# The pooling branch of a hybrid encoder kernel: channels on partitions, shifted sums on GpSimd, map folded into the output weights

## The chip, the core and the metric

The kernel runs on one core of a Trainium2 chip. A core has five engines that run their own instruction streams and meet at semaphores: TensorE (PE, with its weight loads shown as PEld), VectorE (DVE), ScalarE (ACT), GpSimd (POOL) and SyncE (SP), which here only issues transfers. The metric is the device time of one execution in microseconds (us), less is better.

## What is computed

Two layers over 2048 tokens of 1024 channels, float32. Each layer adds a mixing block and an expert block to x. The mixing block has three branches side by side: attention (512 channels), pooling (256) and retention (256), from one projection of h. The pooling branch is what the change is about:

```python
def multiscale_pool(u, pool_w, pool_scale):          # u = the 256 pooling channels of the projection
    cs = jnp.cumsum(uf, axis=1)
    for gi, w in enumerate(POOL_WINDOWS):            # 2, 4, 8, 16: one window for each 64 channels
        shifted = jnp.pad(c, ((0, 0), (w, 0), (0, 0)))[:, :s]
        mean = (c - shifted) / jnp.minimum(t1, float(w))
        outs.append(mean - uf[..., sl])
    y = jnp.einsum('bsgc,gce->bsge', d, pool_w).reshape(b, s, POOL_WIDTH)
    return y * pool_scale

x = x + jnp.einsum('bse,ed->bsd', concatenate([y_a, y_b, y_c]), w_out[l])   # reference, l = layer
x = x + moe_ffn(rms_norm(x, norm_ffn[l]), ...)       # 32 experts, 2 for each token
```

So each pooling channel gets the mean of its last w tokens minus the token itself, then a 64 x 64 map for each group, then a scale, and then its rows of w_out.

## The kernel before

Each layer has a mixing part and an expert part. The **mixing part** goes over 16 tiles of 128 tokens in 18 steps (`steps`): 0 and 1, a hardware loop of six passes over two steps each (2 to 13), then 14 to 17. Step s holds three strands, each a block of code in every engine's stream, woven by hand: *front* projects tile s, *back* mixes tile s-1, *tail* routes tile s-2. `b` is the parity of s, `o` the other one. Nothing but the written order and the semaphores sets what runs when.

TensorE in a full step, in its order: transposes of q, k and the rotated retention heads (`tr`, helper line 1126, which waits for `rank_read`, `qk_ready` and `rope_ready`); `chunk(0)`, the first 512 columns of the projection, as 8 products of hT (stationary) with `win`, line 1151; scores (1201, 1210, 1214); transposes of the routed tile; `chunk(1)`, columns 512 to 1023: k and v in its first 256, the pooling channels u in its last 256; router products (1225); half of `chunk(2)`; the router's fold (1230); retention state (1237); **the pooling bands** (1247 to 1251): u as the stationary operand, with a constant band matrix of window means minus identity as the moving one, `pool_cur` for this tile and `pool_prev` for the last 15 tokens of the tile before, kept in `upv`; retention's inner product (1257, end `pe_ykv`); the other half of `chunk(2)`; transposes of the probabilities; **the pooling map** (1269) after `kvd_read`; half of `chunk(3)`; attention's product with v (1282); transposes of the retention output; rest of `chunk(3)`; the output projection (1305), 8 products for each half k of the 1024 columns, with the ranking products (1162, 1163) between the halves.

VectorE copies the band products to `dT` (line 896), and ScalarE the map's output to `mixT` with the scale (line 713), which ends in `pool_ready`. ScalarE evicts each chunk to `proj`, with the token's normalization `rf` as its scale (lines 679, 691, 705, 717); tokens lie on partitions there. VectorE's rest of the step goes: `kv`, `rstd` (a reciprocal root in 12 short instructions, lines 778 to 789) and z for retention, `route` (962 to 998), `ycT`, squares, `rstd` and scaling for q and k (916 to 924), x addition of half 0 (938), hT of the next tile (818), `place` (1005 to 1018, with `rank_read` at its end), x addition of half 1.

GpSimd does yc (545) when z is ready, six rotary operations (556 to 562), the copy of the tile's last u rows to `upv` (565), at whose end `rope_ready` stands, the copies of v to `v0w` (570, 572), and later the two indirect writes of slots (580), when `slots_ready` has come.

At a layer's start SyncE loads constants (layer 1 only), x, the small parameters, the four parts of w_in, w_out and the next x tiles in one queue. The **expert part** works through 32 experts with all weights streamed; it is the same in both kernels.

## Time and profile before

| | |
|---|---|
| median of 3 runs | 3359.57 us (3357.9 to 3360.9) |
| profiled execution | 3360.36 us, span 3358.6 us |
| TensorE busy | 3213.6 us, 96% |
| VectorE, ScalarE, GpSimd busy | 1488.1, 596.2, 1072.1 us |
| mean granted TensorE clock | 0.979 |
| mixing parts | from 16.37 to about 880 us and from about 1690 to 2550 us |

The span is the time between the first and the last instruction of the profiled execution. In a timeline row stand the start in us from the span's start, the duration, the engine, the line in kernel.py, the operation, output and inputs with their shapes, how many instructions are merged in the row, and in brackets how long the engine was idle before it and what ended that. A float32 product of the program shows as two TensorE instructions. `<-issue` is idle time in which the engine waited for nothing that the profile shows. DVEq, SPq and the like are an engine's instruction queue.

### The profile page before, as it was taken

The page shows a single profiled execution, that of the slowest core. Times are in us where ns is not written, and L with a number is a line of the kernel's source. Part 1 is how long each engine was busy: PE and PEld are TensorE (multiplying, and loading weights), DVE is VectorE, ACT ScalarE, POOL GpSimd, SP SyncE. Part 2 cuts the span into 40 slices and gives each one's busy share as a digit, 9 for nine tenths or more (in the row PEclk, how much of TensorE's full clock was granted, in tenths as well). Part 3 has the DMA queues.
Part 4 walks back from the last instruction along what each step waited for, and adds up shares of the span by engine and source line. Part 5 has one row for each costly group of instructions (what it writes and reads, how often), then busy time and mean ns, then how long its engine had stood idle before and what let it go on. Part 6 is the DMA issues. An engine that isn't in the chain of part 4 may idle for free.

```text
span 3358.6 us, 58551 instructions
## 1 busy us (share of the span) xinstructions
PE 3213.6 (96%) x19892; PEld 2412.3 (72%) x19892; DVE 1488.1 (44%) x4766; ACT 596.2 (18%) x1738; POOL 1072.1 (32%) x1088
## 2 busy tenths in 40 slices
PE   7999999999699999999889999999986999999998
PEld 3555555554499999999845555555554999999998
DVE  3666666666322222222246666666653222222221
ACT  1222222222111111111112222221220111111111
POOL 1111111111155455554310111111111555555543
PEclk9999999999799999999999999999987999999999
DMA  8212112121388899999842122121123889999996
GB/s 281 70 35 69 51 53 69 35 69 64 149 285 280 297 321 328 334 348 341 283 141 70 41 63 69 35 69 59 45 110 147 251 280 319 307 340 334 333 342 189
DMA packets 228590, 613.55 MB, mean 183 GB/s; under 512 B 63724, under 2 KB 120556, under 8 KB 195388
## 3 DMA queue, kind: packets, MB, share of 16 engines
q1 hardware_dynamic: 165724, 527.54, 43.3%
q0 software_dynamic: 62592, 82.75, 11.3%
q8 instruction: 124, 2.03, 0.2%
q14 instruction: 150, 1.23, 0.1%
HBM read 530.95 MB, written 80.35 MB: 182 GB/s over the span
## 4 chain that ended last, share of the span: by engine, by line
PE 84%; DMA 5%; DVE 3%; issue 3%; SPq 1%; DVEq 1%; POOL 1%; ACT 1%; POOLq 0%; ACTq 0%
PE bank L1151 24%; PE bank L1337 23%; PE bank L1365 15%; PE bank L1305 13%; DMA arena<-hrows,arena 3%; PE bank L1126 3%; PE bank L1257 1%; DVE arena L1071 1%; PE bank L1282 1%; PE bank L1201 1%; PE bank L1210 1%; DMA arena<-in_x 1%; PE bank L1225 0%; POOL arena L618 0%; ACT arena L743 0%
## 5 line engine op out<-in xcount | busy, mean ns | idle before, releaser
L1337 PE MATMUL bank<-arena,wts 128*128 128x135 f32 (+6 forms) x8192 | 1022.9, 287 | 3.3 <-ACTq L736 3.3
L1337 PEld LDWEIGHTS bank<-arena,wts 128*128 128x128 f32 x8192 | 1016.6, 191 | 3.5 <-issue 3.5
L1151 PE MATMUL bank<-wts,arena 128*128 128x512 f32 x2048 | 917.7, 597 | 39.5 <-DVE arena L818 20.3
L1151 PEld LDWEIGHTS bank<-wts,arena 128*128 128x128 f32 x2048 | 376.3, 191 | 452.1 <-issue 427.6
L625 POOL DMA_INDIRECT out<-arena x316 | 502.4, 1590 | 157.9 <-issue 89.6
L1365 PE MATMUL bank<-arena,wts 128*128 128x135 f32 (+6 forms) x4096 | 519.4, 287 | 14.7 <-DVE arena L1104 14.3
L1365 PEld LDWEIGHTS bank<-arena,wts 128*128 128x128 f32 x4096 | 511.5, 191 | 18.1 <-issue 18.0
L1305 PE MATMUL bank<-wts,arena 128*128 128x512 f32 x1024 | 454.8, 597 | 0.1
L1071 DVE STREAM_TRANSPOSE arena<-arena 128x256 f32<-128x256 f32 x304 | 135.4, 446 | 559.6 <-DMA arena<-hrows,arena 538.1
L1305 PEld LDWEIGHTS bank<-wts,arena 128*128 128x128 f32 x1024 | 192.9, 191 | 231.8 <-issue 215.6
L618 POOL DMA_INDIRECT arena<-hrows,arena x304 | 294.6, 969 | 183.2 <-issue 163.1
L545 POOL TENSOR_TENSOR arena<-arena 128x256 f32<-128x256 f32 x32 | 23.1, 723 | 950.2 <-DVEq L907 950.2
L1085 DVE STREAM_TRANSPOSE arena<-bank 128x480 f32<-128x480 f32 (+4 forms) x192 | 104.2, 593 | 475.9 <-PE bank L1365 475.9
L743 ACT ACTIVATE arena<-arena,tab 128x256 f32<-128x256 f32 x316 | 133.1, 496 | 616.5 <-DVEq L1086 616.5
L580 POOL DMA_INDIRECT table<-pay,sloti x64 | 63.7, 995 | 457.0 <-DVE sloti L1018 447.2
L613 POOL TENSOR_TENSOR arena<-tab,quarter 128x5 int32<-128x5 int32 (+2 forms) x64 | 12.3, 192 | 426.4 <-DMA tab<-table 377.8
L751 ACT ACTIVATE arena<-bank 128x270 f32<-128x270 f32 (+6 forms) x64 | 26.3, 412 | 649.5 <-PE bank L1337 649.5
L1126 PEld LDWEIGHTS bank<-cst,arena 128*128 128x128 f32 x896 | 103.0, 143 | 44.8 <-issue 38.3
L1126 PE MATMUL bank<-cst,arena 128*128 128x128 f32 x896 | 125.5, 281 | 2.5 <-DVE arena L938 1.6
L722 ACT ACTIVATE arena<-arena 128x1024 bf16<-128x1024 f32 x32 | 33.8, 1056 | 443.3 <-DVE arena L938 443.3
L938 DVE TENSOR_TENSOR arena<-arena,bank 128x512 f32<-128x512 f32 x64 | 44.0, 688 | 116.5 <-PE bank L1305 106.3
L686 ACT ACTIVATE arena<-bank,stat 128x128 f32<-128x128 f32 x256 | 89.8, 380 | 28.2 <-DVEq L864 28.2
(173 smaller groups left out, 2402.1 us busy)
## 6 DMA issues: line engine op xcount, KB each, us to landing
wts<-in_w_gate SPq DMA_DIRECT2D x128, 1024.0 KB, 8.0
wts<-in_w_up SPq DMA_DIRECT2D x128, 1024.0 KB, 10.3
wts<-in_w_down SPq DMA_DIRECT2D x128, 1024.0 KB, 14.7
hrows<-arena SPq DMA_DIRECT2D x36, 512.0 KB, 3.0
out<-arena SPq DMA_DIRECT2D x36, 512.0 KB, 2.7
arena<-in_x SPq DMA_DIRECT2D x32, 512.0 KB, 5.1
wts<-in_w_in SPq DMA_DIRECT2D x8, 2048.0 KB, 15.7
arena<-out SPq DMA_DIRECT2D x32, 512.0 KB, 4.4
```

What stands on the lines that cost most here:

```text
L580: e.indirect_dma_start(table, bass.IndirectOffsetOnAxis(ap=sloti[b][:, k:k + 1].bitcast(U32), axis=0), pay[b][:, 2 * k:2 * k + 2], None).t ...
L618: e.indirect_dma_start(xg[b][:, g * PIECE:(g + 1) * PIECE], None, hpieces, bass.IndirectOffsetOnAxis(ap=piece[:, i, g:g + 1].bitcast(U32), ...
L625: e.indirect_dma_start(opieces, bass.IndirectOffsetOnAxis(ap=piece[:, i, g:g + 1].bitcast(U32), axis=0), ysb[b][:, g * PIECE:(g + 1) * PIE ...
L686: a(pr[:, k, g], (bC, bD)[k][:, g * P:(g + 1) * P], ACT.Exp, bias=stat[:, 16 + n:17 + n], scale=1.0, accum_out=stat[:, 24 + n:25 + n])
L743: a(y, y, ACT.Copy, scale=tab[:, i, g, 1:2].bitcast(F32)).then_inc(y_scaled, 1)
L1071: v.transpose(windows(xT_all[b], g * step, DC, 32 * GMAX, 32), x_piece)
L1085: v.transpose(y[:, 3 * k:3 * k + m], windows(bk, 0, m, w, w))
L1126: return nc.tensor.transpose(dst, src, ident[0:m, 0:m])
L1151: i = mm(bIP[n % 2][:, :], hT[:, d], win[:, n, d], start=(d == 0), stop=(d == DC - 1))
L1305: i = mm(bIP[k][:, :], mixT[:, d], wout[:, d, 512 * k:512 * k + 512], start=(n == 0), stop=(n == DC - 1))
L1337: return mm(gu_at(f, k, w), lhs, xT[:, d, 0:w], start=start, stop=(d == DC - 1), skip_group_check=True)
L1365: j = mm(dst, lhs, hTm[:, f, 0:w], start=(f == 0 and d % 3 == 0), stop=(f == FC - 1), skip_group_check=True)
```

## The change

In seven parts. (a) In chunk 1 the 256 pooling columns are no longer computed with tokens on partitions: for each of 8 slices d there is one product of 256 columns (k and v) and two of 128 with `win` stationary and hT moving, so that u comes out with channels on partitions, unnormalized. ScalarE copies it to `raw_uT`, after a new wait for `pool_ready` of the tile before, and evicts the other half to `proj`. (b) The normalization is per token, and so along the columns now: VectorE writes diag(rf) in place of an empty instruction, TensorE multiplies a matrix of ones with it, ScalarE copies the product to `rfb`. (c) GpSimd keeps 16 columns of the tile before, multiplies by rfb, adds shifted copies for windows 2, 4, 8 and 16, scales by 1/w and subtracts u; the result `dT` (now two) is what the output projection reads. (d) The band products, the map's products, the copies behind them and the copy to `upv` are gone. (e) VectorE multiplies the maps by the scale once a layer, TensorE multiplies them into rows 512 to 767 of w_out in step 1 (`fold`), and ScalarE writes the result over `wout` (`folded`). (f) The constants lose 1536 columns of 128 x 4 bytes and gain 34. (g) `logits4` gets a place of its own.

```diff
-for _name, _n in (("ident", P), ("before", P), ("ones", P), ("causal", P), ("pool_cur", 4 * P),
-                  ("pool_first", 4 * P), ("pool_prev", 4 * P), ("gamma", 2), ("fold", 32), ("rev8", 8),
+for _name, _n in (("ident", P), ("before", P), ("ones", P), ("causal", P),
+                  ("per_window", 2), ("early", 32), ("gamma", 2), ("fold", 32), ("rev8", 8),
...
@@ GpSimd, front
                         e.tensor_tensor(dst[:, :, 1], rtmp[:, 2], rtmp[:, 3], ALU.add)
-                        e.drain()
-
-                        e.tensor_copy(upv[b][96:128, :], proj[b][96:128, U0:U0 + UW]).then_inc(rope_ready, 1)
-                        e.drain()
+                        e.drain().then_inc(rope_ready, 1)
 
                         if back:
                             wait_alone(e, pe_pv, t0)
                         e.tensor_copy(v0w[b][0:64, :], proj[b][0:64, V0:V0 + KVW])
                         e.drain()
                         e.tensor_copy(v0w[o][64:128, :], proj[b][64:128, V0:V0 + KVW]).then_inc(vw_ready, 1)
+                        e.drain()
+
+                        if isinstance(s, int) and s == 0:
+                            e.memset(uT[:, :, 0:16], 0.0)
+                        else:
+                            e.tensor_copy(uT[:, :, 0:16], uT[:, :, P:P + 16])
+                        e.drain()
+                        wait_alone(e, rfb_ready, t0 + 1)
+                        e.tensor_tensor(uT[:, :, 16:], raw_uT, rfb.unsqueeze(1).to_broadcast([P, 2, P]), ALU.mult)
+                        e.drain()
+                        e.tensor_tensor(sums[:, :, 1:], uT[:, :, 1:], uT[:, :, 0:P + 15], ALU.add)
+                        e.drain()
+                        e.tensor_tensor(sums2[:, :, 3:], sums[:, :, 3:], sums[:, :, 1:P + 14], ALU.add)
+                        e.drain()
+                        e.tensor_tensor(sums[:, 1, 7:], sums2[:, 1, 7:], sums2[:, 1, 3:P + 12], ALU.add)
+                        e.drain()
+                        e.tensor_tensor(sums2[64:128, 1, 15:], sums[64:128, 1, 15:], sums[64:128, 1, 7:P + 8], ALU.add)
+                        e.drain()
+                        for ph, total in ((slice(0, 64), sums), (slice(64, P), sums2)):
...
+                            e.tensor_tensor(dT[b][ph], total[ph, :, 16:],
+                                            const("per_window", ph.start, ph.stop).unsqueeze(2).to_broadcast([64, 2, P]), ALU.mult)
+                        e.drain()
+                        e.tensor_tensor(dT[b], dT[b], uT[:, :, 16:], ALU.subtract).then_inc(pool_ready, 1)
                         e.drain()
@@ ScalarE
+                def folded(j):
+
+                    e.wait_ge(pe_fold, l * 2 + j + 1)
+                    for k in range(2):
+                        a(wout[:, 4 + j, 512 * k:512 * k + 512], (bA, bB)[k][:, :], ACT.Copy)
+                    e.drain().then_inc(fold_ready, 1)
...
                         a(proj[b][:, 0:512], bIP0[:, :], ACT.Copy, scale=rf[b]).then_inc(proj_ready, 1)
+                        if isinstance(s, int) and s == 1:
+                            folded(0)
...
                         e.wait_ge(proj_psum, t0 * 4 + 2)
-                        a(proj[b][:, 512:1024], bIP1[:, :], ACT.Copy, scale=rf[b]).then_inc(proj_ready, 1)
+                        if not isinstance(s, int) or s > 0:
+                            e.wait_ge(pool_ready, t0)
+                        a(raw_uT.rearrange("p j n -> p (j n)"), bIP1[:, 256:512], ACT.Copy)
+                        a(proj[b][:, 512:768], bIP1[:, 0:256], ACT.Copy, scale=rf[b]).then_inc(proj_ready, 1)
+                        if isinstance(s, int) and s == 1:
+                            folded(1)
...
                     if front:
+                        e.wait_ge(pe_rfb, t0 + 1)
+                        a(rfb, bA[:, 384:512], ACT.Copy).then_inc(rfb_ready, 1)
                         e.wait_ge(proj_psum, t0 * 4 + 3)
...
-                        e.wait_ge(pe_lin, t0)
-                        for j in range(2):
-                            a(mixT[:, 4 + j], bB[:, j * P:(j + 1) * P], ACT.Copy, scale=pscale[:, j:j + 1])
-                        e.drain().then_inc(pool_ready, 1)
@@ VectorE
-                e.nop().then_inc(rf_ready, 1)
+                v.tensor_scalar(diag[b], ident, rf[b], None, ALU.mult).then_inc(rf_ready, 1)
...
+                v.tensor_tensor(pw, pw, bc(pscale.unsqueeze(2), [P, 2, P]), ALU.mult).then_inc(maps_ready, 1)
...
-                        v.tensor_copy(dT, bB[:, 256:512].rearrange("p (j n) -> p j n", j=2))
@@ TensorE
-                        for d in range(*part):
-                            i = mm(bIP[n % 2][:, :], hT[:, d], win[:, n, d], start=(d == 0), stop=(d == DC - 1))
+                        if n == 1:
+                            for d in range(DC):
+                                mm(bIP1[:, 0:256], hT[:, d], win[:, 1, d, 0:256], start=(d == 0), stop=(d == DC - 1),
+                                   skip_group_check=True)
+                                for j in range(2):
+                                    i = mm(bIP1[:, 256 + P * j:384 + P * j], win[:, 1, d, 256 + P * j:384 + P * j], hT[:, d],
+                                           start=False, stop=(d == DC - 1), skip_group_check=True)
+                        else:
+                            for d in range(*part):
+                                i = mm(bIP[n % 2][:, :], hT[:, d], win[:, n, d], start=(d == 0), stop=(d == DC - 1))
...
+                    def fold(j):
+
+                        e.wait_ge(wout_full, (l + 1) * 16)
+                        e.wait_ge(maps_ready, l + 1)
+                        if j > 0:
+                            e.wait_ge(fold_ready, l * 2 + j)
+                        for k in range(2):
+                            i = mm((bA, bB)[k][:, :], pw[:, j], wout[:, 4 + j, 512 * k:512 * k + 512], start=True, stop=True)
+                        i.then_inc(pe_fold, 1)
+
                     chunk(0)
+                    if first:
+                        fold(0)
...
                     chunk(1)
+                    if first:
+                        fold(1)
...
+                    if front:
+                        if first:
+                            e.wait_ge(fold_ready, l * 2 + 2)
+                        e.wait_ge(rf_ready, t0 + 1)
+                        mm(bA[:, 384:512], ones, diag[b], start=True, stop=True).then_inc(pe_rfb, 1)
...
-                        wait_alone(e, kvd_read, t0)
-                        for j in range(2):
-                            i = mm(bB[:, P * j:P * j + P], pw[:, j], dT[:, j], start=True, stop=True)
-                        i.then_inc(pe_lin, 1)
...
-                                i = mm(bIP[k][:, :], mixT[:, d], wout[:, d, 512 * k:512 * k + 512], start=(n == 0), stop=(n == DC - 1))
+                                i = mm(bIP[k][:, :], dT[o][:, d - 4] if d in (4, 5) else mixT[:, d], wout[:, d, 512 * k:512 * k + 512], start=(n == 0), stop=(n == DC - 1))
```

TensorE's order in a full step of the loop, from the router products to the second half of chunk 2 and to the pooling map, before and then after (the line numbers of after are its own):

```order
L1225 MATMUL bank<-arena,par 32x128 x8
L1149 ISA
L1151 MATMUL bank<-wts,arena 128x512 x4
L1230 MATMUL bank<-cst,arena 128x32
L1237 MATMUL bank<-arena 64x64 x4
L1249 MATMUL bank<-cst,arena 64x128 x2
L1251 MATMUL bank<-cst,arena 64x128 x2
L1249 MATMUL bank<-cst,arena 64x128 x2
L1251 MATMUL bank<-cst,arena 64x128 x2
L1257 MATMUL bank<-arena 128x64 x4
L1151 MATMUL bank<-wts,arena 128x512 x4
L1126 MATMUL bank<-cst,arena 128x128 x8
```

```order
L1183 MATMUL bank<-arena,wts 128x128 x2
L1275 MATMUL bank<-arena,par 32x128 x8
L1177 ISA
L1187 MATMUL bank<-wts,arena 128x512 x4
L1284 MATMUL bank<-arena,cst 128x128
L1286 MATMUL bank<-cst,arena 128x32
L1292 MATMUL bank<-arena 64x64 x4
L1299 MATMUL bank<-arena 128x64 x4
L1187 MATMUL bank<-wts,arena 128x512 x4
L1154 MATMUL bank<-cst,arena 128x128 x8
L1177 REGISTER_ALU
```

The eight band products (1249, 1251) are gone, the product of ones with diag (1284) stands ahead of the router's fold, and chunk 1 ends in products of 128 columns (1183).

GpSimd's order in the same step, from the last rotary operation to the writes of slots, before and then after:

```order
L561 TENSOR_TENSOR arena<-arena 128x8x32
L562 TENSOR_TENSOR arena<-arena 128x8x32
L565 COPY arena<-arena 32x256
L570 COPY arena<-arena 64x128
L572 COPY arena<-arena 64x128
L331 REGISTER_ALU
L580 DMA table<-pay,sloti 69888x2 x2
```

```order
L554 TENSOR_TENSOR arena<-arena 128x256
L559 COPY arena<-arena 64x128
L561 COPY arena<-arena 64x128
L567 COPY arena<-arena 128x2x16
L324 REGISTER_ALU
L570 TENSOR_TENSOR arena<-arena 128x2x128
L572 TENSOR_TENSOR arena<-arena 128x2x143
L574 TENSOR_TENSOR arena<-arena 128x2x141
L576 TENSOR_TENSOR arena<-arena 128x137
L578 TENSOR_TENSOR arena<-arena 64x129
L585 TENSOR_TENSOR arena<-arena,cst 64x256 x2
L588 TENSOR_TENSOR arena<-arena 128x256
```

Nine operations and one wait (for `rfb_ready`) now stand between the v0w copies and the writes of slots, and the copy of u's last rows (565) is gone.

## Rows read from the trace of the kernel before

**Rows 1.** Windows: stretch, busy us (instructions) of PE, PEld, DVE, ACT, POOL, clock, DMA, GB/s

```profile
1780.00:1900.00 120.00, 119.93 (x544) 62.80 (x543) 80.69 (x284) 30.93 (x101) 15.75 (x24) 1.00 0.19 57
```

**Rows 2.** Timeline, TensorE, a full step: start us, us, engine, line, op, shapes, count, idle

```profile
421.64 7.03 PE L1151 MATMUL bank<-wts,arena 128*128 128x512 f32 x16
...
432.95 0.45 PE L1237 MATMUL bank<-arena 128*64 128x64 f32 x8
433.23 0.39 PE L1249 MATMUL bank<-cst,arena 128*64 128x128 f32 x4
...
434.20 1.10 PE L1257 MATMUL bank<-arena 128*128 128x64 f32 x8
...
439.51 0.61 PE L1269 MATMUL bank<-arena,par 128*128 128x128 f32 x4
439.96 3.60 PE L1151 MATMUL bank<-wts,arena 128*128 128x512 f32 x8
...
455.45 7.11 PE L1305 MATMUL bank<-wts,arena 128*128 128x512 f32 x16
```

**Rows 3.** Timeline, TensorE, expert part, then the page's weight loads (mean ns)

```profile
1575.96 7.38 PE L1365 MATMUL bank<-arena,wts 128*128 128x128 f32 x64 [0.26 <-DVE arena L1104]
1583.18 14.46 PE L1337 MATMUL bank<-arena,wts 128*128 128x128 f32 x128
...
L1337 PEld LDWEIGHTS bank<-arena,wts 128*128 128x128 f32 x8192 | 1016.6, 191 | 3.5 <-issue 3.5
```

**Rows 4.** Timeline, GpSimd, the same step as rows 2

```profile
440.37 0.72 POOL L545 TENSOR_TENSOR arena<-arena 128x256 f32<-128x256 f32 x1 [29.46 <-DVEq L907]
...
460.74 1.02 POOL L580 DMA_INDIRECT table<-pay,sloti  x1 [13.69 <-DVE sloti L1018]
```

**Rows 5.** Timeline, VectorE: the same step, loop's edge first; last two: step 16

```profile
418.83 0.69 DVE L842 COPY arena<-bank 128x512 f32<-128x512 f32 x1 [2.47 <-issue]
...
441.23 0.58 DVE L969 TENSOR_TENSOR arena<-arena 128x16 f32<-128x16 f32 x1
...
445.69 0.17 DVE L981 TENSOR_SCALAR arena<-arena 128x8 f32<-128x8 f32 x1
...
459.43 0.19 DVE L1016 CUSTOM_DVE_ANT_0 arena<-arena 128x32 f32<-128x32 f32 x1
...
849.69 0.17 DVE L969 TENSOR_TENSOR arena<-arena 128x16 f32<-128x16 f32 x1
...
852.33 0.17 DVE L981 TENSOR_SCALAR arena<-arena 128x8 f32<-128x8 f32 x1
```

**Rows 6.** Timeline, VectorE and then GpSimd, step 0 of layer 1; last: rows 2's step

```profile
41.96 1.13 DVE L921 TENSOR_TENSOR arena<-arena,stat 128x512 f32<-128x512 f32 x1
...
42.51 1.17 POOL L559 TENSOR_TENSOR arena<-arena 128x256 f32<-128x256 f32 x1
...
455.09 0.69 DVE L921 TENSOR_TENSOR arena<-arena,stat 128x512 f32<-128x512 f32 x1
```

**Rows 7.** Timeline, ScalarE, eviction of chunk 1 in the step of rows 2

```profile
428.71 0.69 ACT L691 ACTIVATE arena<-bank,stat 128x512 f32<-128x512 f32 x1 [1.48 <-PE bank L1151]
```

**Rows 8.** Timeline, TensorE, step 16 of layer 1

```profile
840.39 0.64 PE L1249 MATMUL bank<-cst,arena 128*64 128x128 f32 x4
...
842.24 1.54 PE L1257 MATMUL bank<-arena 128*128 128x64 f32 x8
```

**Rows 9.** Timelines, TensorE, ScalarE, TensorE; then transfers from 0 to 150 us

```profile
66.59 3.70 PE L1151 MATMUL bank<-wts,arena 128*128 128x512 f32 x8 [2.75 <-ACT arena L679]
...
64.82 1.06 ACT L656 ACTIVATE arena<-arena 128x1024 bf16<-128x1024 f32 x1 [15.86 <-DMA arena<-in_x]
...
1720.76 0.66 PE L1126 MATMUL bank<-cst,arena 128*128 128x128 f32 x4 [0.92 <-POOL arena L565]
...
GB/s 158 296 347 387 387 386 387 320 317 386 407 413 409 415 418 405 263 172 11 0 0 9 0 2 0 0 25 115 251 276 106 0 2 0 0 4 0 0 2 0
...
cst<-in_consts SPq DMA_DIRECT2D x1, 1154.0 KB, 5.4
```

52 lines of the change are left out of this document (18 added, 34 removed).

## Prediction

> **What bounds the kernel now.** I read the windows first, to see which engine has no room, then TensorE's timeline of one step of the mixing part, then VectorE's and GpSimd's at the same place, then the ends of each layer. In 120 us in the middle of layer 2's mixing part TensorE is busy for 119.93, at a granted clock of 1.00, that is 2.4 GHz, and the DMA share is 0.19 [rows 1]. So in this part a microsecond taken off TensorE is a microsecond of time, as long as no other engine is late. The mixing part has 18 steps per layer: step s projects tile s ("front"), mixes tile s-1 ("back") and routes tile s-2 ("tail"). Fourteen per layer (s = 2 to 15) are the full kind that rows 2 show, 28 in all. The expert part holds nothing that the change touches; it starts when the mixing part's chain is through, so it only moves.
>
> **What leaves TensorE, per full step.** The pooling band products start at 433.23, and the products after them (line 1257) at 434.20 [rows 2]: four groups like the first, 0.22 each by their spacing, 0.88, plus 0.09 of a gap before line 1257, which I leave standing. The pooling map (line 1269) starts at 439.51 and the next work at 439.96: 0.45 [rows 2]. Together -1.33.
>
> **What comes to TensorE, per full step.** Chunk 1 had 8 products of 512 columns, each shown as two instructions, 16 in 7.03 us: 0.439 each [rows 2]. Now it is 16 instructions of 256 columns and 32 of 128, the same number of columns, but three weight loads where there was one. A 128-column instruction with a fresh weight load takes (1583.18 - 1575.96) / 64 = 0.113 in the expert part [rows 3]. No row shows 256 columns; the line between 0.113 and 0.439 gives 0.221. Sum 16 x 0.221 + 32 x 0.113 = 7.15, so +0.12. Bounds: nothing, if columns alone count; at most 32 x (0.191 - 0.113) = +2.5 more, if each short instruction had to wait for a whole weight load, whose own mean is 0.191 [rows 3]. I stay at +0.12, because rows 3 are the very same shape and hide the load. The product of ones with diag adds two 128-column instructions, 0.23. In all -1.33 + 0.12 + 0.23 = **-0.98 per full step, 28 times: -27.4**.
>
> **GpSimd and VectorE.** GpSimd loses one small copy, which `rope_ready` had to wait for, and gains nine operations behind the v0w copies, from about 446.5 on. A TENSOR_TENSOR of 256 columns takes 0.72 [rows 4]; taking a fixed 0.17 or so and the rest by columns (my estimate), those of 286, 282, 137 and 129 columns cost 0.78, 0.77, 0.47 and 0.46; with four of 256 columns (the product with rfb, two scalings by 64 partitions, the subtraction) and the small copy it is 5.6 us, some 7 with the drains. GpSimd ends near 454, and its next wait, for slots, ends at 460.74 [rows 4]. The output products want dT one step later. GpSimd itself has room.
>
> What it does to VectorE is the dear question. Beside GpSimd's six rotary operations the routing from line 969 to line 981 takes 445.69 - 441.23 = 4.46 us; alone, in the step without them, 852.33 - 849.69 = 2.64, of which about 0.33 is a gap without a releaser [rows 5]. So some 2.15 are lost to six operations, 0.36 each: an addition of 16 columns takes 0.58 instead of 0.17, ending with GpSimd's operation. It goes both ways: a product of VectorE takes 1.13 for 0.69, and GpSimd's beside it 1.17 for 0.72 [rows 6]. The Trainium skill, SBUF — State Buffer, section "SBUF: two separate sides", calls the port pair that these two share an exclusive lock held for the whole instruction; the trace agrees with that, and the GPSIMD Engine Reference, section 4.1, advises against elementwise work on GpSimd.
>
> Eight long operations at 0.36 are 2.9 us. Some of them will lie beside work that rows 5 do not have: a 0.8 us reduction and a copy from PSUM, which showed no stretch, and a 0.8 us square that loses at most one operation for its own length. Walking the two queues against each other by these rules I get 1.8 to 2.3; I take 2.3, with ends at 1.5 and at 5.6, where all of GpSimd's time is lost to VectorE.
>
> The cover is this. VectorE's last step of `place` ends at 459.62, and TensorE's second half of the output products, which starts at 455.45 and takes 7.11, ends at 462.5 [rows 2, 5]. That leaves 2.9. TensorE now reaches this point 0.45 earlier, and VectorE drops the dT copy, about 0.3, and has its 0.2 of diag at another place: **cover 2.7**. TensorE's next step opens with a wait for `rank_read`, behind which the transposes and chunk 0 are queued, so every microsecond beyond 2.7 would be paid, in each of 28 steps. At 2.3 nothing is. The picks for the ranking and hT for chunk 0 are further from being missed. Where the loop of two steps closes, VectorE stands 2.47 without a releaser at the back edge of the loop before line 842, and TensorE waits a few tenths for it [rows 5]; this chain hangs on the end of the output products and stays.
>
> **ScalarE.** It loses two activations for the map's output, gains the copy of rfb, and evicts chunk 1 in two halves, some 0.3 longer. It has 1.48 idle ahead of that eviction [rows 7], and the logits behind it are wanted by TensorE only after half of chunk 2. The new wait for `pool_ready` ahead of raw_uT's copy is over some 20 us earlier. Nothing on the path.
>
> **The ends.** Step 16 has no chunk to hide in, and its pooling products run at twice the time: from 840.39 to 842.24, 1.85 less the gap of 0.1, on the chain [rows 8]: -1.75 twice, **-3.5**. The map there lies beside VectorE's longer way to z and gives nothing. Layer 2: step 0 pays 0.12 + 0.23; step 1 saves 0.44 (half the bands), 0.45 and pays 0.35; the fold is four products of 512 columns, 4 x 0.88 = 3.5, and its evictions (four of 0.69, by the row of the same size in [rows 7]) lie beside chunk 2; the wait of 0.92 for the dropped copy goes [rows 9]. 0.35 - 0.54 + 3.5 - 0.92 = **+2.4**. Layer 1: the same, but its start is bound by transfers. TensorE stands for 2.75 in step 1 because ScalarE gets its x tile only at 64.82, and the queue is full until then (rates by slices of 3.75 us) [rows 9]; the constants shrink from 1154 KB [rows 9] by 1536 - 34 columns, 0.77 MB, 2 us at the 390 GB/s of that stretch [rows 9]. The fold fills the hole, and ScalarE's two evictions of fold 0, some 1.3 us ahead of the exponentials, eat most of the 2 us on the chain to z. I put **0**; ends -1.5 and +2.
>
> **Sum:** -27.4 - 3.5 + 2.4 + 0 = -28.5. The profiled execution took 3360.36 with a span of 3358.6, 0.8 above the median of 3359.57, so I take the sum off the median: **3331**.
>
> **Rivals.** (1) VectorE a little late: a loss of 0.36 for each of eight long operations and a little more, 3.2, is 0.5 beyond the cover: +14, 3345. For it: the plain average of rows 5. Against: the reductions. (2) **VectorE becomes the bound, slower than before:** it decides at a loss of 2.7 + 0.98 = 3.7 per step. If the twelve short operations of the rsqrt each meet a fresh GpSimd operation, 0.6 of each 0.72 may be lost, 4.8 in all: 2.1 beyond the cover, +59 - 28.5, 3390. Against it: rows 5, where two or three of VectorE's operations get through between GpSimd's, and the drains between the sums, which open more room. The lock rule named above, taken to its end, with all of GpSimd's 5.6 us lost, would give (5.6 - 2.7 - 0.98) x 28, about +54, and so nearly the same, 3410. (3) The swapped products of chunk 1 are dear: if a quarter of a weight load showed, 32 x 0.048 = 1.5 per step, 30 steps, +46: 3377; rows 3 speak against it. (4) It doesn't shorten the step, because another chain closes up behind TensorE (the loop's back edge, or ScalarE, whose 1.48 idle before its eviction are not much): 3357. Against: 119.93 of 120. (5) More than thought: the 0.09 gaps go too, chunk 1 costs nothing, the start gains 2: 3323.
>
> **Chances.** Forecast, 3326 to 3337: 0.62. Rival 1, to 3350: 0.16. Rival 2: 0.06. Rival 3: 0.04. Rival 4: 0.07. Rival 5: 0.05. The range from 3323 to 3346 takes in the forecast, rival 5 and most of rival 1. This kernel's times can tell about 0.2%, 6.7 us. Faster by more: 0.83; within: 0.07; slower: 0.10.
>
> **What would show it.** In the trace of after: from line 1292's first product to line 1299's about 0.37 instead of 1.25; chunk 1 in about 7.15; each full step 1 us shorter; no TensorE wait at the start of a step for VectorE's `place`, and VectorE through with `place` only some tenths before it. Rival 1 and 2 show as a TensorE wait there, with stretched rsqrt operations; rival 3 as a chunk 1 of 8 us or more. A wait on wout at the first fold would spoil layer 1's zero.

## The result, and the profile after

| | before | after |
|---|---|---|
| median | 3359.57 us (3 runs; 4 beside the changed kernel: 3359.6) | 3338.77 us (4 runs, 3336.51 to 3344.82) |
| ratio | | 0.9941, 95% interval 0.9927 to 0.9955 |
| profiled execution, span | 3360.36, 3358.6 us | 3337.25, 3335.4 us |

The changed kernel is faster by 20.8 us by the medians, and by 23.2 us between the two profiled spans. The forecast was 28.5, so the time lies 8 us above the predicted 3331. That is inside the range, but 1.8 above the band of the forecast itself (3326 to 3337), in the one that the prediction gave to rival 1. Two more comparisons of the same kernel gave 0.9941 and 0.9953.

Where the time went is read by cutting both traces at the same product, the retention state (line 1237 before, 1292 after), and at the first product of each part. All in us:

| stretch | before | after | measured | forecast |
|---|---|---|---|---|
| span's start to first chunk | 16.37 | 16.44 | +0.1 | -2 to 0 |
| layer 1: first chunk to state of step 2 | 105.04 | 106.97 | +1.9 | 0 with the row above |
| 13 steps to the state of step 15 | 673.95 | 661.92 | -12.0 | -12.7 |
| step 15 to 16 | 44.55 | 43.22 | -1.3 | -1.0 |
| step 16 to expert part | 55.91 | 55.28 | -0.6 | -1.75 |
| expert part of layer 1 | 794.03 | 795.63 | +1.6 | 0 |
| layer 2: first chunk to state of step 2 | 101.58 | 106.09 | +4.5 | +2.4 |
| 13 steps | 673.76 | 661.69 | -12.1 | -12.7 |
| step 15 to 16 | 44.55 | 43.22 | -1.3 | -1.0 |
| step 16 to expert part | 56.24 | 55.34 | -0.9 | -1.75 |
| expert part of layer 2 to the end | 792.6 | 789.6 | -3.0 | 0 |

So 26.8 of the 27.4 forecast for the 28 full steps came. The two starts took back 6.5 where 2.4 was forecast, the two ends of the mixing parts gave 1.5 where 3.5 was forecast, and the expert parts, which are the same code, differ by 1.4 in sum. In the ten kernels that have the change's chunk 1 and its sums on GpSimd at most once, the 13 steps take 661.7 to 663.1, so the trace of after is among the shortest: 0.84 to 0.94 us per step, by the one trace of the kernel before.

The window that answers [rows 1] is this one of after, with the same columns:

```profile
1780.00:1900.00 120.00, 119.79 (x587) 70.13 (x586) 85.27 (x300) 27.85 (x86) 31.36 (x49) 1.00 0.16 49
```

TensorE is still full at a clock of 1.00. GpSimd has gone from 15.75 to 31.36 us and VectorE from 80.69 to 85.27, 4.6 more in 2.4 steps, although VectorE has less to do.

TensorE's timeline of a full step of after, answering [rows 2]:

```profile
424.70 0.64 PE L1275 MATMUL bank<-arena,par 128*32 128x128 f32 x16
425.28 3.70 PE L1187 MATMUL bank<-wts,arena 128*128 128x512 f32 x8
428.81 0.39 PE L1284 MATMUL bank<-arena,cst 128*128 128x128 f32 x2
429.04 0.31 PE L1286 MATMUL bank<-cst,arena 128*128 128x32 f32 x2
429.27 0.45 PE L1292 MATMUL bank<-arena 128*64 128x64 f32 x8
429.65 1.10 PE L1299 MATMUL bank<-arena 128*128 128x64 f32 x8
...
434.08 1.04 PE L1154 MATMUL bank<-cst,arena 128*128 128x128 f32 x8
434.96 3.60 PE L1187 MATMUL bank<-wts,arena 128*128 128x512 f32 x8
...
450.45 7.11 PE L1343 MATMUL bank<-wts,arena 128*128 128x512 f32 x16
457.40 1.25 PE L1154 MATMUL bank<-cst,arena 128*128 128x128 f32 x10
```

From the state to the inner product it is 429.65 - 429.27 = 0.38 where it was 1.25. Between the transposes of the probabilities and chunk 3 the map is gone. The product of ones with diag(rf), line 1284, costs 429.04 - 428.81 = 0.23. No row waits. Chunk 1, from another full step of after:

```profile
111.72 0.60 PE L1180 MATMUL bank<-wts,arena 128*128 128x256 f32 x2
112.16 0.61 PE L1183 MATMUL bank<-arena,wts 128*128 128x128 f32 x4
112.60 0.60 PE L1180 MATMUL bank<-wts,arena 128*128 128x256 f32 x2
...
118.84 0.64 PE L1275 MATMUL bank<-arena,par 128*32 128x128 f32 x16
```

Eight such pairs of rows take 118.84 - 111.72 = 7.12 us; before, the same place took 6.97 (110.10 to 117.07).

GpSimd and VectorE in the same step of after; the first three rows are GpSimd's, where [rows 4] had an empty engine, the others VectorE's, answering [rows 5]. Last, by itself, stands the row of before that the last row of after answers:

```profile
441.80 0.21 POOL L567 COPY arena<-arena 128x32 f32<-128x32 f32 x1
...
445.97 1.30 POOL L585 TENSOR_TENSOR arena<-arena,cst 64x256 f32<-64x256 f32 x2
447.40 1.13 POOL L588 TENSOR_TENSOR arena<-arena 128x256 f32<-128x256 f32 x1
...
443.43 0.47 DVE L980 SCALAR_TENSOR_TENSOR arena<-arena,stat,cst 128x32 f32<-128x32 f32 x1
...
446.77 1.17 DVE L944 TENSOR_TENSOR arena<-arena 128x640 f32<-128x640 f32 x1
...
449.66 0.17 DVE L813 TENSOR_TENSOR newton<-newton 128x10 f32<-128x10 f32 x1
...
456.89 0.17 DVE L1046 CAST sloti<-arena 128x2 int32<-128x2 f32 x1
457.60 0.69 DVE L966 TENSOR_TENSOR arena<-arena,bank 128x512 f32<-128x512 f32 x1 [0.55 <-PE bank L1343]
```
```profile
462.60 0.69 DVE L938 TENSOR_TENSOR arena<-arena,bank 128x512 f32<-128x512 f32 x1 [2.68 <-PE bank L1305]
```

The pooling takes GpSimd from 441.80 to 448.53, 6.7 us with its drains (forecast: some 7). Beside it an operation of VectorE on 32 columns takes 0.47 instead of 0.25, and the 640-column square 1.17 where it took 0.81 in before. It ends at 447.94, and GpSimd's subtraction (1.13 instead of 0.72) only at 448.53. The pooling is over 1.1 us before the reciprocal root's short operations with two inputs begin, which run at their usual 0.17. VectorE ends `place` at 457.06, and TensorE's next transposes start at 457.40: 0.3 to spare.

### The profile page after: what moved, and what is told of

Same layout as the page of the kernel before. It is cut to its first block, busy times and chain, and to the rows that moved or that the text cites. A ratio compares the mean times of both kernels' runs of the same rounds, so it can differ in the third digit from the quotient of the medians.

```text
span 3335.4 us, 60077 instructions
## 1 busy us (share of the span) xinstructions
PE 3189.2 (96%) x20372; PEld 2502.4 (75%) x20372; DVE 1535.5 (46%) x4768; ACT 590.2 (18%) x1746; POOL 1233.5 (37%) x1346
## 3 DMA queue, kind: packets, MB, share of 16 engines
q14 instruction: 152, 1.25, 0.1%
## 4 chain that ended last, share of the span: by engine, by line
PE 87%; DMA 4%; DVE 3%; issue 3%; SPq 2%; DVEq 1%; POOL 1%; ACT 1%; ACTq 0%; POOLq 0%
PE bank L1375 25%; PE bank L1187 18%; PE bank L1403 15%; PE bank L1343 13%; PE bank L1183 3%; PE bank L1180 3%; PE bank L1154 3%; DMA arena<-hrows,arena 2%; PE bank L1299 1%; PE bank L1320 1%; PE bank L1249 1%; DVE arena L1099 1%; PE bank L1258 1%; PE bank L1275 0%; DMA arena<-in_x 0%
## 5 line engine op out<-in xcount | busy, mean ns | idle before, releaser
L1375 PEld LDWEIGHTS bank<-arena,wts 128*128 128x128 f32 x8192 | 1017.1, 191 | 3.4 <-issue 3.4
L1187 PE MATMUL bank<-wts,arena 128*128 128x512 f32 x1536 | 694.7, 599 | 37.9 <-DVE arena L847 20.8
L1187 PEld LDWEIGHTS bank<-wts,arena 128*128 128x128 f32 x1536 | 281.3, 191 | 341.0 <-issue 320.9
L1403 PEld LDWEIGHTS bank<-arena,wts 128*128 128x128 f32 x4096 | 510.9, 191 | 18.6 <-issue 18.2
L1343 PE MATMUL bank<-wts,arena 128*128 128x512 f32 x1024 | 453.6, 596 | 0.3 <-DVE arena L940 0.2
L1343 PEld LDWEIGHTS bank<-wts,arena 128*128 128x128 f32 x1024 | 192.5, 191 | 231.2 <-issue 214.8
L1183 PEld LDWEIGHTS bank<-arena,wts 128*128 128x128 f32 x1024 | 154.5, 191 | 13.1
L1183 PE MATMUL bank<-arena,wts 128*128 128x128 f32 x1024 | 155.5, 274 | 0.0
L1180 PE MATMUL bank<-wts,arena 128*128 128x256 f32 x512 | 153.1, 381 | 0.0
L1154 PE MATMUL bank<-cst,arena 128*128 128x128 f32 x896 | 126.4, 283 | 1.6 <-DVE arena L966 1.6
```

The source lines that it names most:

```text
L1154: return nc.tensor.transpose(dst, src, ident[0:m, 0:m])
L1180: mm(bIP1[:, 0:256], hT[:, d], win[:, 1, d, 0:256], start=(d == 0), stop=(d == DC - 1), skip_group_check=True)
L1183: i = mm(bIP1[:, 256 + P * j:384 + P * j], win[:, 1, d, 256 + P * j:384 + P * j], hT[:, d], start=False, stop=(d == DC - 1), skip_group_ch ...
L1187: i = mm(bIP[n % 2][:, :], hT[:, d], win[:, n, d], start=(d == 0), stop=(d == DC - 1))
L1343: i = mm(bIP[k][:, :], dT[o][:, d - 4] if d in (4, 5) else mixT[:, d], wout[:, d, 512 * k:512 * k + 512], start=(n == 0), stop=(n == DC - 1))
L1375: return mm(gu_at(f, k, w), lhs, xT[:, d, 0:w], start=start, stop=(d == DC - 1), skip_group_check=True)
```

## Experiments

The twelve kernels below form three groups of four, in the order in which they stand here. Each group ran on one chip, beside the kernel before on that chip, which took 3387.85 us in the first group, 3362.07 in the second and 3419.96 in the third. So ratios and times are compared within a group. "To step 2" is the second row of each layer in the table above.

### The changed kernel again

> The changed kernel once more, as it is, so that the edits sent with it have a partner on the same chip. Theory (the step is bound by TensorE, 0.92 us shorter, the rest given back at the layer starts): 3337 to 3341, a ratio to before near 0.994.

3368.22 us, 0.9941 of before (0.9927 to 0.9955). The stretches repeat: 662.89 and 662.69 for the 13 steps, 107.67 and 105.36 to step 2. The absolute time was another chip's.

### Without the fold

```diff
                     chunk(0)
-                    if first:
-                        fold(0)
...
                     chunk(1)
-                    if first:
-                        fold(1)
```

and without ScalarE's `folded` and the waits for it. The maps then don't reach the output: the pooling channels go through w_out unmapped.

> The fold into the output weights is left out (products, evictions, waits), so the pooling map isn't applied. Theory: in layer 2 the four products cost their 3.5 us in full; in layer 1 they no longer fit wholly into the hole of 2.75 us in step 1, since the constants brought the x tile no earlier, so they cost 1 to 2 there: 4.5 to 5.5 less than the changed kernel, 3333 to 3336. Rival (the fold hides in layer 1, as forecast, and the missing microseconds are elsewhere): 3.5 less.

4992.96 us, and that says nothing: other values reach the router, and TensorE runs twice as many products in each expert part, an extra round of experts. Only the mixing parts compare. To step 2 it is 105.63 instead of 107.67 in layer 1 and 102.52 instead of 105.36 in layer 2, so leaving it out gives 2.0 and 2.8; in layer 2 the granted clock differs too, and at the same clock it is 3.4 (see the account of layer 2's start below). In layer 1 the hole stays without it, here in TensorE's timeline:

```profile
67.58 3.70 PE L1183 MATMUL bank<-wts,arena 128*128 128x512 f32 x8 [2.30 <-ACT arena L702]
```

### GpSimd's sums twice

```diff
+                        for again in range(2):
-                        e.tensor_tensor(sums[:, :, 1:], uT[:, :, 1:], uT[:, :, 0:P + 15], ALU.add)
+                            e.tensor_tensor(sums[:, :, 1:], uT[:, :, 1:], uT[:, :, 0:P + 15], ALU.add)
...
```

down to the scaling by `per_window`: six operations more, 3.5 us, and their drains.

> GpSimd does the four sums and the two scalings twice (same values, 3.5 us more of work in each step with a front). Theory (the cover of VectorE was 2.7, 2.1 of it is used, 0.55 is left): the second set falls on the short operations of the rsqrt, each of six loses up to 0.45, 2.7 in all, 2.1 beyond what is left, so about 2 us per step in 28 steps: +45 to +70 over the changed kernel, 3385 to 3410, with a TensorE wait for VectorE at the start of steps. Rival (VectorE isn't near the bound, the lock costs nothing that matters): within 3 us of the changed kernel.

3396.55 us, 1.0027 of before (1.0015 to 1.0039): 28 us slower than the changed kernel on the same chip, where 45 to 70 was expected; 13 steps in 675.23 instead of 662.89, 0.95 more per step instead of 2. The expected price was too high, the mechanism is there. In this kernel's waits from 100 to 820 us (engine and line, for whom: us in total, times, longest), and in TensorE's timeline:

```profile
PE bank L1155 <- DVEq L1046: 11.8, 13, 1.1
```
```profile
465.31 1.28 PE L1155 MATMUL bank<-cst,arena 128*128 128x128 f32 x10 [0.93 <-DVEq L1046]
```

TensorE waits once in every step for the `drain` of VectorE that raises `rank_read` (line 1046 of this kernel, ahead of the last row of `place`). With the 0.3 that VectorE had to spare, 3.5 us more on GpSimd delayed VectorE by 1.2 to 1.3. The second set of sums lies beside the reciprocal root: its twelve short operations and the starts between them take 4.3 us here and 2.9 in the changed kernel. Six of them keep their 0.17, the others take 0.23 to 0.59.

### Without the sums

```diff
-                        e.tensor_tensor(sums[:, :, 1:], uT[:, :, 1:], uT[:, :, 0:P + 15], ALU.add)
...
-                        e.tensor_tensor(dT[b], dT[b], uT[:, :, 16:], ALU.subtract).then_inc(pool_ready, 1)
+                        e.tensor_tensor(dT[b], uT[:, :, 0:P], uT[:, :, 16:], ALU.subtract).then_inc(pool_ready, 1)
```

The window means are left out; dT is a difference of two tokens.

> The four sums and the two scalings are left out, dT is the difference of shifted columns (the means are missing), so GpSimd does 3.5 us less in each step. Theory (GpSimd's work is under cover): the time stays that of the changed kernel, within 3 us, and VectorE's idle time before the second x addition grows from 0.55 to 1.5 or more. Rival (the port costs TensorE something in each step already): 0.3 us or more per step, 8 or more less.

3366.81 us, 0.9934 (0.9918 to 0.9949), 1.4 us under the changed kernel; 13 steps in 662.20. VectorE's idle time ahead of the second x addition is 1.6 instead of 0.6 (means over the layer), as expected:

```profile
460.77 0.69 DVE L950 TENSOR_TENSOR arena<-arena,bank 128x512 f32<-128x512 f32 x1 [1.55 <-PE bank L1327]
```

Six fewer operations on GpSimd give VectorE 1.0 us and TensorE nothing in the steps: the cover holds, and with the run above it is placed between the present load and 3.5 us more of it.

### Constants as long as before

```diff
+            e.dma_start(wts[:, 16384:16384 + 12 * P - 34], w_out[0:1, 0:256, ...]).then_inc(consts_full, 16)
             e.dma_start(cst[:, :], consts_d).then_inc(consts_full, 16)
```

with all waits for the constants raised to both: the 0.77 MB that the change saves are moved after all.

> A transfer of 0.77 MB that nothing needs is put ahead of the constants, and all engines wait for both, so that as many bytes as in the kernel before precede the first weights. Theory now (the first 16 us are not bound by bytes): within 1 us of the changed kernel and the first product within 1 us of 16.4. Rival (the forecast's: bytes at 390 GB/s): 2 us more.

3342.46 us, 0.9940 (0.9923 to 0.9956). First product at 17.23, to step 2 107.10. The 0.77 MB are worth 0.8 us at the start at the most, and less than the difference between two runs of the same kernel (16.44, 17.05, 16.83).

### Chunk 1 with the old operands

```diff
-                        if n == 1:
+                        if n == 99:
```

Chunk 1 is computed with tokens on partitions, so GpSimd works on the wrong layout; the amount of work elsewhere is the same.

> Chunk 1 keeps the operand order of the kernel before, so u stands with tokens on partitions and the pooling takes the wrong axis; all else as in the changed kernel. Theory: 0.15 less in each of 32 steps, 4.8 less than the changed kernel. Rival (the three weight loads cost more than the timeline shows): 10 or more less.

3332.61 us, 0.9918 (0.9901 to 0.9934). The 13 steps take 660.58 and 660.94 instead of 662.64 and 662.36 in the kernel with long constants beside it: the many short products cost 0.11 to 0.16 per step, forecast 0.12. The whole time is 9.9 us below that kernel and 6.7 below the early fold of the same group, not 4.8, and by the number alone the rival stands. Between the traces of this kernel and the one with long constants, 6.7 of the difference lie in the two expert parts. Other values reach the router here too, so that these parts do not compare, and what makes them shorter is not shown.

### The kernel before without its pooling

The band products, the copy to dT and the map's products are taken out of the kernel before; ScalarE copies the maps to mixT in place of the pooled channels.

> The kernel before without its pooling bands, its dT copy and its map products (ScalarE scales the map weights instead, so the pooling branch is missing). It prices the part that removes. Theory: 0.88 + 0.45 in 28 steps, 0.9 in two, 1.75 in each step 16: 37.2 + 1.8 + 3.5 = 42 less than before, 3317. If the given-back part lies in the removal itself (other waits close up): 30 or less.

3319.59 us, 0.9875 (0.9858 to 0.9891), 42.5 less. 13 steps take 656.83: 1.32 less per step than before's 673.95, against 0.88 + 0.45 = 1.33 in the forecast. This is all that could be had by removing, and the change gets 20.8 of it, half: chunk 1, the rfb product and the fold are new, and the starts and ends of the mixing parts give back more than was forecast.

### Early fold in layer 2

```diff
                 with e.If(l > 0):
                     load_par()
+                    load_wout()
                     wait_alone(e, x_adds, h0 * 2 + 1)
                     load_pieces(0)
```

and, in layer 2 only, both folds ahead of the first chunk on TensorE, both `folded` ahead of the first squares on ScalarE. Layer 1 is as in the changed kernel.

> The changed kernel, but in layer 2 w_out is loaded as soon as the last expert is through, and the fold is done while TensorE waits for the first tile (19.95 us); layer 1 keeps it in step 1. Theory: 3.5 us of products leave the path in layer 2, and TensorE starts the layer with a higher clock, another 1: 4 to 5 less than the changed kernel, 3333 to 3336. Rival (the transfer of 4 MB delays the x tile and the last weights by as much): no gain or up to 8 more.

3339.29 us, 0.9933 (0.9917 to 0.9950), against 0.9940 for the kernel with long constants beside it: 3.2 us less by the medians where 4 to 5 was expected, and the two kernels' runs overlap. TensorE's timeline of this kernel:

```profile
1679.17 3.78 PE L1177 MATMUL bank<-wts,par 128*128 128x512 f32 x4 [18.03 <-DMA wts<-in_w_out]
1684.15 3.49 PE L1177 MATMUL bank<-wts,par 128*128 128x512 f32 x4 [1.20 <-ACTq L683]
1687.48 7.03 PE L1210 MATMUL bank<-wts,arena 128*128 128x512 f32 x16
```

The fold does lie at the low clock, and chunk 0 then runs at full clock, 7.03 for its 16 instructions. But w_out now stands ahead of the x tile in the queue, and chunk 0 starts 3.7 later behind the first expert transposes of layer 1, against the 6.2 by which the way from there to step 2 is shorter (99.56 instead of 105.73). The third group measures this again. Layer 1, whose code is that of the changed kernel, took 110.14 to step 2 here; the account of layer 1's start below says why.

### The partner, late padding, halves, and both

> The changed kernel once more, as the partner of the three beside it. Expected: 0.994 of the kernel before, and in layer 1 some 107 us from the first product to the first retention-state product of step 2 (106.97 in the run on record, 107.10 and 107.67 in two others).

3404.32 us, 0.9953 (0.9940 to 0.9967). To step 2: 108.35 and 104.92.

**Late padding.** The writes of padding (line 418 and the two after it in the changed kernel) go behind step 1's loads:

```diff
+                def pads():
                     with e.If(l == 0):
...
                     if front and not back:
                         rest()
+                    if isinstance(s, int) and s == 1:
+                        pads()
```

> The changed kernel with the writes that clear the padding (eight of 512 KB to hrows and out, and the 546 KB of the table) issued behind step 1's loads of x and of the rotary table instead of ahead of them; nothing else moves. Theory A: in layer 1 the x tile for step 2 lands at 64.8 us only because it stands in the queue behind w_out and 4.6 MB of padding, and the fold, put into step 1, was to fill the hole that this leaves; at the 0.40 MB per us that the profile shows there, the tile lands 11 us earlier, at about 54, the hole of some 2.7 us ahead of the transposes of step 1 goes, and the way to step 2 takes 104 to 105 us instead of 107: 2 to 3 us in all. Theory B: the start of the layer is set by the weights and the chain of products, and the hole only moves to the next wait (for ScalarE's or VectorE's copies): under 0.7 us. Either way nothing changes in the steady steps or in layer 2.

3399.72 us, 0.9939 (0.9925 to 0.9952), 4.6 less than its partner, and no run of the one reaches into those of the other (3399.24 to 3400.68, 3403.62 to 3405.83). The same kernel's ratio to before moved from 0.9941 to 0.9953, some 4 us, between the first group and this one, so the size of the gain is uncertain. ScalarE's timelines: the squares of the x tile for step 2, first in the partner, then with late padding; then TensorE's second half of the fold, in the same order:

```profile
66.55 1.06 ACT L672 ACTIVATE arena<-arena 128x1024 bf16<-128x1024 f32 x1 [15.75 <-DMA arena<-in_x]
```
```profile
54.01 1.06 ACT L675 ACTIVATE arena<-arena 128x1024 bf16<-128x1024 f32 x1 [4.07 <-DMA arena<-in_x]
```
```profile
69.33 1.98 PE L1228 MATMUL bank<-wts,par 128*128 128x512 f32 x4 [1.77 <-ACTq L681]
71.15 3.60 PE L1187 MATMUL bank<-wts,arena 128*128 128x512 f32 x8
```
```profile
67.07 1.88 PE L1231 MATMUL bank<-wts,par 128*128 128x512 f32 x4
68.79 3.60 PE L1190 MATMUL bank<-wts,arena 128*128 128x512 f32 x8
```

The tile comes 12.5 us earlier, the wait of 1.77 is gone, and the state of step 2 comes at 122.83 instead of 125.18, 2.35 us earlier. From the first product it is 106.51 instead of 108.35, 1.8 less. So theory A's mechanism is there, and more than the 0.7 of theory B, but the 104 to 105 that A said were not reached. The rest of the 4.6 (1.2 in the expert part of layer 1, some in that of layer 2) is not told from scatter.

> The early fold of layer 2 again (w_out loaded ahead of the x tile, both folds ahead of the first input chunk), now with the fold's products cut to the blocks of the map that are not zero: 64x64 blocks instead of 128x128, two side by side in rows and columns of the array, eight products of 64 rows instead of four of 128. If TensorE runs the two blocks side by side, the fold takes half of its 3.5 us at full clock in both layers: 1.8 us less in layer 1, and in layer 2 nothing more than the early fold gave, since there it lies under the wait for the first x tile. If the two blocks run one after the other, layer 1 gains nothing. The whole against the changed kernel: 2 to 6 us less by the first, 1 to 3 by the second.

3401.09 us, 0.9940 (0.9927 to 0.9954), 3.2 less than the partner and inside what was expected, but 2.3 of the 2.7 between the two traces lie in the expert part of layer 2, the same code. Layer 1, second half of the fold, and layer 2, first half, in TensorE's timeline:

```profile
68.24 1.93 PE L1178 MATMUL bank<-wts,par 64*64 64x512 f32 x8 [1.36 <-ACTq L683]
...
1710.18 3.68 PE L1178 MATMUL bank<-wts,par 64*64 64x512 f32 x8 [18.49 <-DMA wts<-in_w_out]
...
1718.76 7.47 PE L1211 MATMUL bank<-wts,arena 128*128 128x512 f32 x16
```

Eight instructions of 64 rows take 1.93 where four of 128 rows took 1.98: the two blocks do run side by side, one after the other they would take 3.5. But that only makes up for their number. The expectation of half the time was a slip: a block needs all 512 columns, as the whole map does. The early fold, in the four kernels of this group:

| | expert part of layer 1 to first chunk | first chunk to step 2 | sum |
|---|---|---|---|
| partner | 826.74 | 104.92 | 931.66 |
| late padding | 825.56 | 105.23 | 930.79 |
| early fold in halves | 833.70 | 100.01 | 933.71 |
| both | 830.81 | 99.95 | 930.76 |

Early folding takes 5 us out of the second column, 3.4 of them the fold and 1.5 the clock (half of it was granted for 0.7 us after the first product instead of 3.7), and puts 5 to 7 into the first. Its sum is not better in either pair.

> Both at once: late padding and the early fold in halves. If the two gains are of different waits they add: late padding 2 to 3 us in layer 1, early fold 1 to 3 in layer 2, so some 4 us less than the changed kernel, 0.992 to 0.993 of the kernel before. If in layer 1 both fill the same hole, the sum is that of the larger one.

3399.31 us, 0.9935 (0.9921 to 0.9949), the same as late padding alone (3399.72); the two do not add. Late padding is the version to keep; the early fold adds nothing to it.

## Why the prediction was right, and where it was off

**The whole, inside the range by its width.** The sum of 28.5 was 8 too large by the medians, and the range holds the time only because it reaches up for rival 1, so there is luck in it. Rival 1 did not happen: no TensorE wait for `place` and no stretched reciprocal root stand in the trace. What was missing lies at the starts and ends of the mixing parts, which rival 1 does not speak of.

**Full steps, right.** 0.925 per step over 26 steps against 0.98, and 1.33 in each of the two from state 15 to state 16, where chunk 1 and the rfb product no longer count. Bands and map: 1.33 forecast, 1.32 by taking them out. rfb: 0.23 and 0.22 to 0.23. Chunk 1: 7.12 against 6.97, so 0.15, forecast 0.12; rival 3 is out by these rows and by the 13 steps with the old operands. The bound by 128-column rows of the expert part [rows 3] was the right neighbour. The missing 0.06 per step is the 0.03 of chunk 1 and a few hundredths that no row shows.

**VectorE, right by mechanism and size.** Idle time of VectorE ahead of the second x addition fell from 2.64 to 0.55 in most steps, a loss of 2.1 against 2.3 forecast (the six sums and scalings, by leaving them out, 1.0 of it), and the loss stopped 0.3 short of costing TensorE anything. Rival 2's mechanism is real: the doubled sums turned it on, and the kernel is slower than before with them. Its price was too high: 4.8 us if each of the root's twelve operations is hit, where six more GpSimd operations beside them cost 1.2 to 1.3. The price of 0.36 for each GpSimd operation was that of operations back to back; the six sums cost 0.17 each, the six extra ones some 0.2. The Trainium skill's exclusive lock (SBUF — State Buffer, section "SBUF: two separate sides"), which the prediction took to its end in rival 2, agrees with the trace for operations that meet: GpSimd's second scaling ends at 447.27, VectorE's square 0.67 later, GpSimd's subtraction 0.59 after that, one behind the other. The step from there to a loss of all of GpSimd's time does not follow: 2.1 were lost to 6.7. That GpSimd is through before the reciprocal root's two-input operations start spared them the stretch that they show with doubled sums.

**Layer 1's start, wrong by 2.** The forecast said that the fold fills the hole of 2.75 [rows 9] and that 0.77 MB less bring everything forward by 2 us. The fold fitted only by half, and the bytes brought nothing. For the bytes: ScalarE's x tile came at 64.78, as before (64.82), and the run with long constants moved the first product by less than the scatter. For the hole, ScalarE's and then TensorE's timeline of after:

```profile
64.78 1.06 ACT L672 ACTIVATE arena<-arena 128x1024 bf16<-128x1024 f32 x1 [15.06 <-DMA arena<-in_x]
65.84 0.67 ACT L702 ACTIVATE arena<-bank,stat 128x512 f32<-128x512 f32 x1
66.41 1.07 ACT L680 ACTIVATE wts<-bank 128x512 f32<-128x512 f32 x2
```
```profile
67.55 1.98 PE L1228 MATMUL bank<-wts,par 128*128 128x512 f32 x4 [0.80 <-ACTq L681]
69.38 3.60 PE L1187 MATMUL bank<-wts,arena 128*128 128x512 f32 x8
```

Only the first half of the fold stands ahead of the wait and fills it. The second needs banks that ScalarE empties in `folded(0)`, and ScalarE gets to that only after the same late x tile: 1.07 for `folded(0)` and 1.83 for the second half are queued behind the hole, and chunk 2 starts at 69.38 instead of 66.59. Less the 0.8 that the way from there to the state of step 2 is shorter, that is the +1.9. I had looked at how much room the hole has, not at which instruction of ScalarE ends it and what the new ones wait for. Late padding, which brings the tile forward, shows it: the second half then waits for nothing.

How late the tile is sets the whole start. In the seven kernels that have the full fold in step 1 and the padding ahead, ScalarE begins on this tile at 64.78 to 67.81, and the state of step 2 comes 58.6 us later in every one (58.62 or 58.63); without the fold it is 56.75, in the kernel before 56.6. So the fold's price here is 1.9 to 2.0, whatever the tile does, and the scatter of 3 us between equal kernels is that of the transfer. With late padding the state came at 122.8 and 122.5, against 123.4 to 126.4 in the seven: its gain is as large as the tile would have been late, 0.6 us against the trace of after and 2.35 against the partner's. First rows of the state of step 2, before and after:

```profile
121.41 0.45 PE L1237 MATMUL bank<-arena 128*64 128x64 f32 x8
```
```profile
123.41 0.45 PE L1292 MATMUL bank<-arena 128*64 128x64 f32 x8
```

**Layer 2's start, too small by 2.1.** Up to the first chunk of step 1 it is 32.50 instead of 31.40, +1.1 where +0.35 - 0.92 was forecast; from there to step 2, with the fold, +3.4 for 2.96. The fold's own price was right: 3.5 forecast, 1.81 + 1.72 by the starts of its rows and of what follows them. What was not foreseen is the clock. Windows of before and then of after, from the first product of chunk 0 on, columns as in [rows 1]:

```profile
1689.85:1691.85 2.00, 2.00 (x3) 0.97 (x4) 1.30 (x10) 0.00 (x0) 0.00 (x0) 0.50 0.33 43
1691.85:1693.85 2.00, 2.00 (x5) 0.88 (x4) 0.61 (x4) 0.00 (x0) 0.00 (x0) 0.69 1.05 353
1693.85:1696.00 2.15, 2.15 (x7) 0.95 (x6) 0.46 (x3) 1.15 (x2) 0.00 (x0) 1.00 1.00 222
```
```profile
1679.46:1681.46 2.00, 2.00 (x3) 0.96 (x4) 1.30 (x10) 0.00 (x0) 0.00 (x0) 0.50 0.46 147
1681.46:1683.46 2.00, 2.00 (x4) 0.87 (x3) 0.82 (x5) 0.59 (x1) 0.00 (x0) 0.50 0.96 292
1683.46:1685.50 2.04, 2.04 (x3) 0.67 (x2) 1.00 (x7) 0.55 (x2) 0.00 (x0) 0.50 1.05 251
```

After 20 us without work TensorE starts at half clock (0.50, 1.2 GHz) in both, but gets the full one some 3 us into chunk 0 before and some 6 us after. By the record of the granted clock it is 3.26 and 6.03 us, and since products take twice as long at half clock (the fold's four instructions 3.49 us there, 1.88 at full clock), the difference costs 1.4. It is no property of the change: six other kernels with the fold in the same place and chunk 1 of the new kind had 3.70 to 5.60 us of half clock and took 104.92 to 105.87 to step 2. Taking half of the time at half clock off (my working from these figures) leaves 103.07 or 103.08 in all seven, 102.60 with the old operands of chunk 1, 99.63 without the fold and 99.96 in the kernel before. So at the same clock the change costs 3.1 in layer 2's start, and the fold 3.4 of its own; the 2.8 that leaving it out gave has a clock difference in it. A wait of 0.30 for hT that before did not have comes up in place of the 0.92. And 0.35 of the excess is in the cut of the table: chunk 1 and the rfb product of step 2 lie ahead of its state, so that this row should read +2.75 and the one from step 15 to 16 -1.33. Then 1.4 for the clock and 0.3 for the wait close the sum: 4.45 against 4.5.

**Step 16, too large by about 1 each.** The bands and more did go: from the state to the product of attention with v it is 1.61 less in layer 1 and 2.03 in layer 2. It was given back behind the last ranking. TensorE's first expert transposes, line 1328 before and 1366 after, both in layer 1:

```profile
895.82 2.58 PE L1328 MATMUL bank<-cst,arena 128*32 128x128 f32 x44 [10.12 <-DMA arena<-hrows,row]
```
```profile
883.83 2.57 PE L1366 MATMUL bank<-cst,arena 128*32 128x128 f32 x44 [10.98 <-DMA arena<-hrows,row]
```

The way from the end of GpSimd's last write of slots over the table in memory and back to the gathered rows took 10.5 instead of 9.6, 0.6 of the difference ahead of the table's arrival, 0.2 ahead of the gather. No line of the change stands there, but it is no scatter either: it is 9.5 to 9.6 in both layers of the two kernels without the new pooling, 10.2 to 10.6 in eight kernels with it, and 9.7 to 10.0 in the other four with it, which leave the fold out or have it early. What does it is open, and with it what the change itself costs there. From the state of step 16 to here, the kernels with the change took 54.5 to 56.1 (two layers each), most of them 55.1 to 55.7, and the kernel before without its pooling 54.78 and 54.31, against 55.91 and 56.24 before. From the state of step 16 to the end of the last write, after takes 1.5 and 1.9 less than before, so the 1.75 of the forecast is in the steps, and the term that it lacked is this 0.9.

**Medians and spans.** The profiled spans differ by 23.2, the medians by 20.8. By the spans 5.3 us are missing: 4.1 at the starts, 2.0 behind step 16, 0.6 in the full steps, less the 1.4 of the expert parts, whose code is the same. The other 2.4 lie between the profiled execution and the median of four that run from 3336.5 to 3344.8, and are not told from scatter.

## What to carry to other kernels

When work is put into a hole on the bound engine, follow the wait that ends the hole: an operation that needs something from the engine which is itself late stands behind the hole, not in it. Elementwise work can go to GpSimd beside VectorE if VectorE has idle time where it matters, counted, by these kernels, at 0.17 to 0.36 us lost for each long GpSimd operation; doubling the suspected load shows how near the edge one is, and here it was near. Before trading for bytes at a kernel's start, look at which transfers stand ahead of the awaited one in the queue: moving 4.6 MB behind it brought a tile 12.5 us forward, and 0.77 MB less at the front brought it nothing. When two starts from idle are compared, take the time at half clock out first: it was 3.0 to 6.0 us here for the same work, and hid 0.6 of the fold's 3.4.

## What the runs showed of the hardware

- A product with 64 rows and 64 columns of weights runs beside another one in the other quadrant of the array: eight instructions of 512 columns in 1.93 us, four of the full size in 1.98.
- Float32 products of 256 columns, which no row of before had: with two of them and four of 128 in turn, a slice of chunk 1 takes 0.87 to 0.88 us, as one product of 512 columns does. Weight loads three times as many (mean 191 ns each) were hidden but for 0.15 us in the whole chunk.
- The low clock after an idle stretch of 20 us held for 3.0 to 6.0 us of the same products (eleven traces), so that equal starts differ by up to 1.5 us.
- Leaving 0.77 MB out of the first transfer moved neither the first product nor the awaited tile. From 3.5 to 7.5 us the core's transfers ran at 230 GB/s after and 310 before, from 7.5 to 12 at 312 and 354: what there was less to move was moved more slowly. With the long constants it was 305 and 328.
